# Running sums moved under the projections, decays read from padded buffers, and the scan's inverse begun by direction

## Chip, core and metric

One core of a Trainium2 chip runs the whole program: TensorE (PE, with its weight loads as PEld), VectorE (DVE), ScalarE (ACT), GpSimd (POOL) and SyncE (SP), which work in parallel and wait for one another by semaphores. The metric is the device time of one execution in microseconds; lower is better. All data is float32.

## What is computed

Two layers of a transformer block with three mixers, then one block of another kind, on 256 tokens of width 1024 with 256 context tokens. The change lies in the second block's recurrence. Cut to what matters:

```
z = centred_shift(z, shift_w)               # a three-token blend per channel
r, k, v, wd, ad, gd = split(z)
w_log = -softplus(-(w0 + tanh(wd) @ w_up)) - 0.5      # per direction
decay = exp(-exp(w_log))
a     = sigmoid(a0 + ad @ a_up)                       # per direction
kk    = head_l2norm(k * k_k);  k_eff = k * (1 + (a - 1) * k_a)
def step(s, (w, kk, a, k, v, r)):           # 16 heads of 64, forward and backward in time
    sa = s @ kk
    s  = s * w - outer(sa, kk * a) + outer(v, k)
    return s, s @ r
```

Four steps' worth of context tokens (64 each) and then four of the input's tokens are scanned; only the latter give an output. Since exp(-exp(w_log)) is exp(-c * sigmoid(..)) with c = exp(-0.5), the product of decays over a span of tokens is the exponential of a running sum of sigmoids.

## The kernel before

The recurrence is computed in chunks of 64 tokens: eight steps h = 0 to 7, each with both directions d (0 forward, 1 backward) side by side in 1024 columns (2 directions x 8 channel blocks x 64 tokens). Steps 4 to 7 are X_STEPS, which also read the state. A step solves a triangular system of 64 x 64 per head and direction, by an inverse that doubles its block size in six levels (LEVELS).

**Projections.** RW_ORDER lists 26 chunks p = 0 to 25 of 128 channels. For each, TensorE multiplies (`rw_chunk`), ScalarE evacuates twice (L2182, L2183), VectorE adds the two shifted neighbours (L2593, L2595). Chunks 2 to 9 are 256 columns wide, 10 to 25 are 512. Behind chunks 4 to 19 stand the 16 rate products (`rates`, n = p - 4): two banks of TensorE, two sigmoids of ScalarE (L2158) into `staged`. After each odd n ScalarE issues two stores (L2163) of that pair to `rates_dram`, and the next pair's sigmoids wait for them, since `staged` has one buffer. Chunks 13 and 17 give VectorE the squares of the keys (`kk_squares`), chunks 15 and 19 the reciprocals of their norms (`kk_inverse_roots`, L2585). PSUM is two rings of four banks, one that ScalarE empties (`act_ring`) and one that VectorE empties (`dve_ring`); TensorE's `open` waits until the bank's last user is done, and `rates` opens two banks before its first product.

**Loading.** Once all 16 stores have landed, SP loads the rates of steps 0 and 1 (L1524), and later those of step h when step h-2 has made its matrices. R0 holds the decay sigmoids of a step, R1 the others.

**A step.** VectorE makes the inclusive running sum of R0 in r2 (`cumulate`, L2560) and the exclusive one, the difference, in r3 (`exclude`). ScalarE turns them into three exponentials: R0 (`first_decays`, L2168), r2 (L2172) and r3 (L2175). GpSimd multiplies them with the keys into Pm, Qm and Km (`removal_raw`, `key_factors`, `removal_keys`, `keys_raw`, `keys`; all L2939). All of this is made for step h+1 during step h; for step 0 during chunks 20 to 25. TensorE then multiplies removal and keys (`together`), VectorE masks the result to LT (`left_matrix`) and Apk (`intra`), ScalarE evacuates the token halves (L2218), GpSimd subtracts the identity (`begin_inverse`) and makes ARm, ScalarE copies its halves crosswise to DTm (`first_transposed`). TensorE makes the right-hand sides U0 (`uncorrected`), which ScalarE evacuates (L2206), in steps 4 to 7 the products Arq and Ark (`reads`), and then runs `inverse`: an identity product per direction, and five rounds of left products and doubled products, in banks held for its whole length. The four banks of the products are those that K and U0 had before.

The order is written out by hand: each engine runs its own list.

## Time and profile before

| what | us |
|---|---|
| median of the runs (lowest, highest of 3) | 2798.57 (2788.01, 2801.04) |
| the profiled execution | 2783.9 |
| its span on the core | 2782.1 |
| TensorE busy | 2546.2 (92%) |
| VectorE, ScalarE, GpSimd busy | 1305.2, 607.6, 510.3 |
| granted TensorE clock, mean | 0.967 |

Busy time is the sum of an engine's instructions; the rest of its span it waits. A granted clock of 1 is 2.4 GHz. In a timeline a row is a run of like instructions: start, time, engine, line of the kernel, operation, tiles, count, and in brackets the idle time before it with what ended it ("<-ACT mem L2206": an instruction of ScalarE at that line; "ACTq" or "DVEq": a drain or semaphore of its queue; "issue": nothing that the profile shows). The projections for the recurrence end at about 1526 us, the scan at about 1936.

### The profile page before, as it was taken

The numbers are of one execution on the slowest core, as the hardware profiler recorded it, in microseconds if no ns is written. First come the engines' busy times: TensorE is split into PE (matmuls) and PEld (weight loads), VectorE is DVE, ScalarE is ACT, GpSimd is POOL, SyncE is SP. The second block draws the span as 40 slices with busy tenths as digits, with TensorE's granted clock in tenths as the row PEclk, the third lists the DMA queues.
The fourth block names the chain that finished last, engine by engine and source line by source line (L and its number), as shares of the span: only waits on it lengthen the run. The fifth ranks groups of instructions, "written<-read, shape, count | busy, mean of one in ns | idle before, by whom it ended". The sixth has DMA issues, their size and how long they took to land.

```text
span 2782.1 us, 51515 instructions
## 1 busy us (share of the span) xinstructions
PE 2546.2 (92%) x22060; PEld 1751.8 (63%) x22060; DVE 1305.2 (47%) x2861; ACT 607.6 (22%) x1348; POOL 510.3 (18%) x402
## 2 busy tenths in 40 slices
PE   8999999999999999998899788898998988877777
PEld 6688785477887844444677788888876533333333
DVE  2873300147631002066347445544217677777666
ACT  2253000014320000115233344332001111111111
POOL 0000000000000000000003544440002454545452
PEclk9999999999999999999999899999999998989999
DMA  5423343343234346215442000002337999999997
GB/s 197 154 96 121 148 155 152 132 172 123 92 121 152 151 151 263 115 61 212 140 132 61 33 17 33 18 3 96 126 127 308 411 420 421 421 421 422 421 421 312
DMA packets 76642, 523.81 MB, mean 188 GB/s; under 512 B 6704, under 2 KB 23088, under 8 KB 28848
## 3 DMA queue, kind: packets, MB, share of 16 engines
q0 software_dynamic: 37056, 269.12, 23.4%
q1 hardware_dynamic: 22768, 243.80, 23.0%
q10 hardware_dynamic: 16640, 8.39, 1.1%
q8 instruction: 126, 2.06, 0.3%
q14 instruction: 52, 0.43, 0.0%
HBM read 511.85 MB, written 9.44 MB: 187 GB/s over the span
## 4 chain that ended last, share of the span: by engine, by line
PE 72%; DVE 12%; DMA 10%; issue 2%; DVEq 2%; ACT 2%; ACTq 0%; POOL 0%; SPq 0%
PE psum L519 35%; PE psum L1562 28%; DMA mem<-weights,mem 8%; PE psum L2007 4%; DVE mem L2889 4%; DVE mem L2393 2%; PE psum L746 2%; PE psum L535 1%; PE psum L1979 1%; DMA rates_dram<-mem 1%; PE psum L1572 1%; DVEq L2514 0%; DVE mem L2847 0%; DVE mem L2530 0%; DVEq L2563 0%
## 5 line engine op out<-in xcount | busy, mean ns | idle before, releaser
L1562 PE MATMUL psum<-mem 64*64 64x64 f32 (+5 forms) x16032 | 935.2, 262 | 78.4 <-ACT mem L2206 17.8
L519 PE MATMUL psum<-mem 128*128 128x256 f32 (+9 forms) x4228 | 966.9, 398 | 4.2 <-ACTq L803 2.1
L1562 PEld LDWEIGHTS psum<-mem 64*64 64x64 f32 (+2 forms) x16032 | 737.6, 147 | 275.1 <-issue 150.6
L519 PEld LDWEIGHTS psum<-mem 128*128 128x128 f32 (+4 forms) x4228 | 706.5, 182 | 256.9 <-issue 168.6
L2007 PE MATMUL psum<-mem 128*128 128x512 f32 x1024 | 496.5, 642 | 124.7 <-ACT mem L2357 121.8
L2007 PEld LDWEIGHTS psum<-mem 128*128 128x128 f32 x1024 | 205.5, 205 | 409.2 <-issue 244.7
L3028 POOL DMA_INDIRECT mem<-weights,mem x256 | 318.3, 1243 | 531.3 <-PE psum L2007 265.7
L2889 DVE CUSTOM_DVE_ANT_0 mem<-mem 128x1024 f32<-128x1024 f32 x256 | 307.4, 1224 | 139.5 <-DMA mem<-weights,mem 132.9
L2939 POOL TENSOR_TENSOR mem<-mem 128x512 f32<-128x512 f32 (+2 forms) x132 | 186.0, 1427 | 649.2 <-PE psum L1562 462.5
L2393 DVE TENSOR_TENSOR mem<-psum,mem 128x512 f32<-128x512 f32 (+1 forms) x193 | 131.0, 683 | 264.7 <-PE psum L1562 239.6
L2393 DVE TENSOR_TENSOR mem<-mem 128x4 f32<-128x4 f32 (+7 forms) x219 | 147.5, 681 | 89.3 <-ACTq L2115 67.5
L2352 ACT ACTIVATE mem<-mem 128x4 f32<-128x4 f32 (+2 forms) x70 | 14.4, 205 | 513.1 <-DVE mem L2893 504.3
L1259 DVE TENSOR_TENSOR mem<-mem 128x512 f32<-128x512 f32 x32 | 22.2, 692 | 193.7 <-ACTq L961 193.7
L1050 DVE SCALAR_TENSOR_TENSOR mem<-mem 128x256 f32<-128x256 f32 x240 | 105.6, 481 | 9.0 <-issue 0.4
L1262 DVE TENSOR_TENSOR mem<-psum,mem 128x512 f32<-128x512 f32 x8 | 5.5, 692 | 205.5 <-PE psum L519 205.5
L1275 POOL DMA_DIRECT2D mem<-vectors x1 | 0.5, 536 | 544.3 <-DVEq L1266 544.3
L1277 POOL MEMSET mem<- 128x256 f32 x1 | 0.3, 311 | 502.0 <-ACT mem L964 502.0
L2357 ACT ACTIVATE mem<-mem 128x128 f32<-128x128 f32 x256 | 82.5, 390 | 32.6 <-DVE mem L2393 31.2
L815 ACT ACTIVATE mem<-psum 128x512 f32<-128x512 f32 (+5 forms) x94 | 48.5, 569 | 105.8 <-PE psum L519 101.8
L960 ACT ACTIVATE mem<-psum 128x512 f32<-128x512 f32 x32 | 19.1, 597 | 201.6 <-PE psum L519 201.6
L2258 ACT ACTIVATE mem<-psum 128x512 f32<-128x512 f32 x64 | 38.2, 597 | 113.0 <-PE psum L1562 110.4
L746 PE MATMUL psum<-mem 128*128 128x512 f32 x128 | 57.5, 608 | 3.8 <-DVEq L1248 3.8
(242 smaller groups left out, 1294.7 us busy)
## 6 DMA issues: line engine op xcount, KB each, us to landing
mem<-weights SPq DMA_DIRECT2D x100, 2048.0 KB, 7.4
rates_dram<-mem ACTq DMA_DIRECT2D x16, 512.0 KB, 7.1
mem<-rates_dram SPq DMA_DIRECT2D x16, 512.0 KB, 5.0
mem<-weights SPq DMA_DIRECT2D x7, 1024.0 KB, 6.8
mem<-weights SPq DMA_DIRECT2D x2, 2176.0 KB
mem<-weights,mem POOLq DMA_INDIRECT x256, 27.2
mem<-weights SPq DMA_DIRECT2D x2, 1536.0 KB, 8.0
mem<-weights SPq DMA_DIRECT2D x2, 1152.0 KB
```

The source lines that it names most:

```text
L519: ins = pe.matmul(out, lhsT, rhs, start=start, stop=stop, skip_group_check=skip)
L746: ins = pe.matmul(b, mg[:, k, t * P:(t + 1) * P], w[half][:, k, :], start=k == 0, stop=k == 7)
L815: return A(dst, src(b) if src else b, func).then_inc(act_ring.free, 1)
L1050: v.scalar_tensor_tensor(cacc[:, c, :], src, w, cacc[:, c, :], ALU.mult, ALU.add)
L1562: ins = pe.matmul(out, lhsT, rhs, start=start, stop=stop, skip_group_check=skip)
L2007: last = pe.matmul(psum[:, 4 + 2 * t + half, :], diag[:, n % DIAGS, :], rows_uv[buf_of[n]][:, D + half * 512:D + (half + 1) * 512], start= ...
L2258: A(Dm[:, d * 512:(d + 1) * 512], banks[2 * d], ACT.Copy)
L2357: A(diag[:, n % DIAGS, :], ident, ACT.Copy, scale=g1[:, n:n + 1]).then_inc(diag_ready.sem, 1)
L2393: return v.tensor_tensor(o, a, b, op)
L2889: v.tensor_tensor_reduce(u, u, h2[:, t, :], 1.0, 0.0, ALU.mult, ALU.add, actp[:, n:n + 1])
L2939: return pool.tensor_tensor(o, a, b, op)
L3028: pool.indirect_dma_start(out=rows_uv[buf_of[n]], out_offset=None, in_=UV, in_offset=bass.IndirectOffsetOnAxis(ap=eidx_u[:, n:n + 1], axis ...
```

## The change

The change does the following. The running sums are made where the sigmoids are staged: VectorE runs one `tensor_tensor_scan` in place per chunk (two rate chunks of one part at a time), two chunks behind the sigmoids; there are two staging buffers, and GpSimd issues the stores once both sums of a pair exist. What the scan loads is already the running sum; its buffers are 65 columns apart and have a column of ones in front of (or behind) each 64, so that the exclusive decay is the inclusive one read one column away. Each step keeps two exponentials, and r3 is gone. In a step GpSimd, ScalarE and TensorE treat the inverse's first level by direction.

```diff
-    rates_in = [sb2(2048, slots_at), lora]
-    R0, R1 = ([buf[:, 1024 * part:1024 * part + 1024] for buf in rates_in] for part in range(2))
-    first_restart = r3[:, 0:512]
-    staged = [yb.rearrange("p c t -> p (c t)")[:, 1024 * part:1024 * part + 1024].rearrange("p (b c n) -> p b c n", b=8, c=2)
-              for part in range(2)]
+    rates_in = [sb2(2 * RATES, slots_at).rearrange("p (s n) -> p s n", s=2), rates_odd.rearrange("p (s n) -> p s n", s=2)]
+
+    def padded(ap, at):
+        return ap[:, at:at + 1040].rearrange("p (d c n) -> p d c n", d=2, n=65)[:, :, :, 0:64]
+
+    R0, R1 = ([padded(buf[:, part, :], 1) for buf in rates_in] for part in range(2))
+    R0_before = [[padded(buf[:, 0, :], 2 * d)[:, d, :, :] for d in range(2)] for buf in rates_in]
+    staging = [yb.rearrange("p c t -> p (c t)"), zv[:, 4:8, :].rearrange("p c t -> p (c t)")]
+    staged = [[buf[:, 1024 * part:1024 * part + 1024].rearrange("p (b c n) -> p b c n", b=8, c=2) for part in range(2)]
+              for buf in staging]
     rates_dram = nc.dram_tensor("rates_dram", (2, 8, P, 2, 8, 64), F32, kind="Internal").ap()
     at_kt = rtop[0] - 7 * 1024
...
@@ -1520,9 +1527,9 @@
                         sp.wait_ge(*intra_ready.at(h - 2, 1))
                     for d in range(2):
                         stream, step = divmod(h, 4)
-                        to = rates_in[h % 2].rearrange("p (s d n) -> p s d n", s=2, d=2)[:, :, d, :]
-                        sp.dma_start(to, rates_dram[d, 4 * stream + (3 - step if d else step)].rearrange("p s c n -> p s (c n)")).then_inc(
-                            rates_landed[h % 2], 16)
+                        for part, to in enumerate((R0, R1)):
+                            sp.dma_start(to[h % 2][:, d, :, :], rates_dram[d, 4 * stream + (3 - step if d else step), :, part]).then_inc(
+                                rates_landed[h % 2], 16)
...
         def reads(h):
-            b = [[dve_ring.open(pe, n) for n in ("Arq", "Ark")] for _ in range(2)]
+            b = []
+            pe.wait_ge(*lt_ready.at(h, 1))
             for d in range(2):
+                b.append([dve_ring.open(pe, n) for n in ("Arq", "Ark")])
+                pe.wait_ge(*qt_ready.at(h, d))
...
-        def inverse(h):
+        def first_left(h, d, left):
+            pe.wait_ge(*inverse_begun.at(h, d))
+            for c in range(8):
+                for head in range(2):
+                    last = tile(left[d], d, c, head, 0, 0, half_of(LT), lambda side, d, c: C2["id2"][64 * side:64 * side + 64, :])
+            last.then_inc(left_full.sem, 1)
+
+        def inverse(h, left):
             products = [[act_ring.open(pe, "held") for _ in range(2)] for _ in range(2)]
-            left = [dve_ring.open(pe, "held") for _ in range(2)]
-            pe.wait_ge(*inverse_begun.at(h))
-            for d in range(2):
-                for c in range(8):
-                    for head in range(2):
-                        last = tile(left[d], d, c, head, 0, 0, half_of(LT), lambda side, d, c: C2["id2"][64 * side:64 * side + 64, :])
-                last.then_inc(left_full.sem, 1)
-            pe.wait_ge(*inverse_begun.at(h, 1))
...
@@ -1921,11 +1931,18 @@
                 pe.wait_ge(*qt_ready.at(h, 0))
                 together(removal(h, 1), keys(h, 0))
                 together(keys(h, 1))
-            pe.wait_ge(*qt_ready.at(h, 1))
-            uncorrected(h)
             if h in X_STEPS:
                 reads(h)
-            inverse(h)
+                uncorrected(h)
+                left = [dve_ring.open(pe, "held") for _ in range(2)]
+                first_left(h, 0, left)
+            else:
+                left = [dve_ring.open(pe, "held") for _ in range(2)]
+                first_left(h, 0, left)
+                uncorrected(h)
+            pe.wait_ge(*qt_ready.at(h, 1))
+            first_left(h, 1, left)
+            inverse(h, left)
@@ -2150,34 +2167,30 @@
 
         def rates(n):
             d, c = divmod(n, 8)
-            if n >= 2 and c % 2 == 0:
-                act.wait_ge(rates_stored, 16 * n)
+            pair = n // 2
+            if pair >= 2 and c % 2 == 0:
+                act.wait_ge(rates_stored, 32 * (pair - 1))
             for part, bias in enumerate(("w0", "a0")):
                 b = take("rate").rearrange("p (b n) -> p b n", b=8)
                 k = 8 * d + c
-                done(A(staged[part][:, :, c % 2, :], b, ACT.Sigmoid, bias=V2[bias][:, k:k + 1]))
-            if c % 2:
-                act.drain().then_inc(rates_staged.sem, 1)
-                act.wait_ge(*rates_staged.at(0, n // 2))
-                for part in range(2):
-                    act.dma_start(rates_dram[d, :, :, part, c - 1:c + 1, :].rearrange("b p c n -> p b (c n)"),
-                                  staged[part].rearrange("p b c n -> p b (c n)")).then_inc(rates_stored, 16)
-
-        def first_decays(h):
-            act.wait_ge(*cumsum_ready.at(h))
-            A(R0[h % 2], r2, ACT.Exp, scale=DECAY)
+                done(A(staged[pair % 2][part][:, :, c % 2, :], b, ACT.Sigmoid, bias=V2[bias][:, k:k + 1]))
+            act.drain().then_inc(rates_staged.sem, 1)
+
+        def decays(h):
+            act.wait_ge(rates_landed[h % 2], 64 * (h // 2 + 1))
+            if h:
+                act.wait_ge(*k_ready.at(h - 1))
+            sums = R0[h % 2].rearrange("p d c n -> p (d c) n")
+            A(ch(r2), sums, ACT.Exp, scale=-DECAY)
             act.drain()
-
-        def removal_decays():
-            A(r2, r2, ACT.Exp, scale=-DECAY)
-
-        def key_decays():
-            A(r3, r3, ACT.Exp, scale=DECAY).then_inc(decays_ready.sem, 1)
+            A(sums, sums, ACT.Exp, scale=DECAY).then_inc(decays_ready.sem, 1)
...
+            if p == 22:
+                act.wait_ge(rates_stored, 16 * STORES)
             dst, w = shift_out(c)
             A(dst, b[:, HALF - w:HALF], ACT.Copy, scale=V2["shift"][:, 26 + c:27 + c])
             done(A(zraw[:, p % 2, HALF - w:HALF], b[:, HALF - w:HALF], ACT.Copy))
...
             key_tokens(h, 1)
-
-        def first_transposed(h):
-            act.wait_ge(*inverse_begun.at(h, 0))
-            A(DTm[64:128, :], ARm[0:64, :], ACT.Copy)
-            A(DTm[0:64, :], ARm[64:128, :], ACT.Copy)
-            act.drain().then_inc(inverse_begun.sem, 1)
-
-        def inverse(h, between):
+            if h in X_STEPS:
+                first_transposed(h, 0)
+            first_transposed(h, 1)
+
+        def first_transposed(h, d):
+            act.wait_ge(*inverse_begun.at(h, d))
+            half = slice(512 * d, 512 * d + 512)
+            A(DTm[64:128, half], ARm[0:64, half], ACT.Copy)
+            A(DTm[0:64, half], ARm[64:128, half], ACT.Copy)
+            act.drain().then_inc(inverseT_ready[d].sem, 1)
+
+        def inverse(h):
             banks = act_ring.held(4)
             for j in range(1, LEVELS):
                 for d in range(2):
...
@@ -2547,27 +2552,24 @@
         def dir_(ap, d):
             return ch2(ap)[:, d, :, :]
 
-        def restarts(to):
-            v.memset(to, 1.0)
-            v.drain()
-            v.memset(to.rearrange("p (c t) -> p c t", c=8)[:, :, 0:1], 0.0)
-            v.drain()
-
-        def cumulate(h, d, restart=restart):
-            s = slice(512 * d, 512 * d + 512)
-            r0 = R0[h % 2]
-            out, decay = (r2[:, s][:, ::-1], r0[:, s][:, ::-1]) if d else (r2[:, s], r0[:, s])
-            v.tensor_tensor_scan(out, restart, decay, 0.0, ALU.mult, ALU.add)
-
-        def exclude(h):
-            v.drain()
-            tt(r3, r2, R0[h % 2], ALU.subtract)
+        def restarts():
+            v.memset(restart, 1.0)
+            v.drain()
+            v.memset(restart.rearrange("p (c t) -> p c t", c=8)[:, :, 0:1], 0.0)
+            v.drain()
+
+        def cumulate(n):
+            pair, part = divmod(n, 2)
+            v.wait_ge(*rates_staged.at(0, 2 * pair + 1))
+            sums = staging[pair % 2][:, 512 * part:512 * part + 512]
+            sums = sums[:, ::-1] if pair >= 4 else sums
+            v.tensor_tensor_scan(sums, restart, sums, 0.0, ALU.mult, ALU.add)
             v.drain().then_inc(cumsum_ready.sem, 1)
 
         def chunk_decay(h):
             v.wait_ge(*decays_ready.at(h))
-            v.tensor_copy(Wnext[:, 0:8], dir_(R0[h % 2], 0)[:, :, 63])
-            v.tensor_copy(Wnext[:, 8:16], dir_(R0[h % 2], 1)[:, :, 0])
+            v.tensor_copy(Wnext[:, 0:8], R0[h % 2][:, 0, :, 63])
+            v.tensor_copy(Wnext[:, 8:16], R0[h % 2][:, 1, :, 0])
             v.drain()
 
         def kk_squares(half):
...
+                cumulate(n)
+            if n == 14:
+                cumulate(14)
+                cumulate(15)
             if p == 20:
                 v.wait_ge(weights.used, used0 + SLOTS + ITEM2["rw4_0"] + 1)
-                restarts(first_restart)
-                v.wait_ge(rates_landed[0], 32)
-                cumulate(0, 0, first_restart)
-                cumulate(0, 1, first_restart)
-            if p == 21:
-                exclude(0)
-            if p == 23:
+                for buf in rates_in:
+                    v.memset(buf[:, 0, 0:520].rearrange("p (c n) -> p c n", n=65)[:, :, 0:1], 1.0)
+                    v.memset(buf[:, 0, 521:1041].rearrange("p (c n) -> p c n", n=65)[:, :, 64:65], 1.0)
+            if p == 24:
                 chunk_decay(0)
-            if p == 24:
                 v.memset(yb, 0.0)
                 v.memset(St, 0.0)
         v.drain().then_inc(state_ready.sem, 1)
...
                 ptt(ch2(LT)[:, d, :, :], ch2(LT)[:, d, :, :], bc(C2["id2"], 1, 8), ALU.subtract)
-            pool.drain()
-            if h:
-                pool.wait_ge(*u_ready.at(h - 1, 1))
-            for d in range(2):
+                pool.drain()
+                if h and d == 0:
+                    pool.wait_ge(*u_ready.at(h - 1, 1))
                 ptt(ch2(ARm)[:, d, :, :], ch2(LT)[:, d, :, :], bc(first[:, d, :], 1, 8), ALU.mult)
-            pool.drain().then_inc(inverse_begun.sem, 1)
-
+                pool.drain().then_inc(inverse_begun.sem, 1)
+
+        for pair in range(8):
+            d, c = divmod(2 * pair, 8)
+            pool.wait_ge(*cumsum_ready.at(0, 2 * pair + 1))
+            for part in range(2):
```

VectorE at chunks 14 and 15 of the projections, before; L2593 and L2595 are the two shifted additions, L2585 the reciprocals, L2393 a product:

```order
L2593 SCALAR_TENSOR_TENSOR mem<-mem 128x2x255 [waits shift_parts_ready]
L2595 SCALAR_TENSOR_TENSOR mem<-mem 128x2x255
L2593 SCALAR_TENSOR_TENSOR mem<-mem 128x2x255 [waits shift_parts_ready]
L2595 SCALAR_TENSOR_TENSOR mem<-mem 128x2x255
L2585 RECIPROCAL mem<-mem 128x512 [waits kk_root_ready,dve_bank_full] x4
L2393 TENSOR_TENSOR mem<-mem 128x2048
```

The same place after; L2566 is a running sum (printed as a SCALAR_TENSOR_TENSOR), L2595 and L2597 are the additions:

```order
L2595 SCALAR_TENSOR_TENSOR mem<-mem 128x2x255 [waits shift_parts_ready]
L2597 SCALAR_TENSOR_TENSOR mem<-mem 128x2x255
L2566 SCALAR_TENSOR_TENSOR mem<-mem 128x512 [waits rates_staged]
L2595 SCALAR_TENSOR_TENSOR mem<-mem 128x2x255 [waits shift_parts_ready]
L2597 SCALAR_TENSOR_TENSOR mem<-mem 128x2x255
L2587 RECIPROCAL mem<-mem 128x512 [waits kk_root_ready,dve_bank_full] x4
L2398 TENSOR_TENSOR mem<-mem 128x2048
L2566 SCALAR_TENSOR_TENSOR mem<-mem 128x512 [waits rates_staged]
```

A running sum stands behind each chunk's additions; that of chunk 15, the second of pair 4, also behind the reciprocals.

TensorE in step 1, from the second removal product with the first keys to the inverse's loop, before; 64x2x64 are removal and key products:

```order
L1562 MATMUL psum<-mem 64x2x64 [waits act_bank_free]
L1562 MATMUL psum<-mem 64x2x64 x15
L1562 MATMUL psum<-mem 64x64 [waits act_bank_free,state_ready,intra_ready,qt_ready]
L1562 MATMUL psum<-mem 64x64 x15
L1562 MATMUL psum<-mem 64x64 [waits term_full,tokens_ready]
L1562 MATMUL psum<-mem 64x64 x31
L1562 MATMUL psum<-mem 64x64 [waits term_full]
L1562 MATMUL psum<-mem 64x64 x15
L1562 MATMUL psum<-mem 64x64 [waits dve_bank_free,act_bank_free,inverse_begun]
L1562 MATMUL psum<-mem 64x64 x31
L1880 UNCONDITIONAL_BRANCH [waits inverse_begun]
```

And after:

```order
L1569 MATMUL psum<-mem 64x2x64 [waits act_bank_free]
L1569 MATMUL psum<-mem 64x2x64 x15
L1569 MATMUL psum<-mem 64x64 [waits inverse_begun,dve_bank_free]
L1569 MATMUL psum<-mem 64x64 x15
L1569 MATMUL psum<-mem 64x64 [waits state_ready,act_bank_free]
L1569 MATMUL psum<-mem 64x64 x15
L1569 MATMUL psum<-mem 64x64 [waits term_full,intra_ready,tokens_ready]
L1569 MATMUL psum<-mem 64x64 x31
L1569 MATMUL psum<-mem 64x64 [waits term_full,intra_ready]
L1569 MATMUL psum<-mem 64x64 x15
L1569 MATMUL psum<-mem 64x64 [waits inverse_begun,qt_ready]
L1569 MATMUL psum<-mem 64x64 x15
```

The identity products (16 for each direction) stood together behind U0 and needed the product banks (act_bank_free); now the first 16 stand before U0's 64, the other 16 behind, and the product banks are opened last.

ScalarE at chunks 5 and 6, before; L2158 are the sigmoids:

```order
L2158 ACTIVATE mem<-psum,mem 128x8x64 [waits act_bank_full] x2
L2163 DMA rates_dram<-mem 128x8x128 [waits rates_staged]
L2163 DMA rates_dram<-mem 128x8x128
L2182 ACTIVATE mem<-psum,mem 128x256 [waits shift_parts_used,act_bank_full]
L2183 ACTIVATE mem<-psum 128x256
L2158 ACTIVATE mem<-psum,mem 128x8x64 [waits act_bank_full,rates_stored]
```

And after, from chunk 6 to chunk 8; L2176 are the sigmoids, L2195 and L2196 the evacuations:

```order
L2176 ACTIVATE mem<-psum,mem 128x8x64 [waits act_bank_full] x2
L2195 ACTIVATE mem<-psum,mem 128x256 [waits shift_parts_used,act_bank_full]
L2196 ACTIVATE mem<-psum 128x256
L2176 ACTIVATE mem<-psum,mem 128x8x64 [waits act_bank_full] x2
L2195 ACTIVATE mem<-psum,mem 128x256 [waits shift_parts_used,act_bank_full]
L2196 ACTIVATE mem<-psum 128x256
L2176 ACTIVATE mem<-psum,mem 128x8x64 [waits act_bank_full,rates_stored]
```

The stores left ScalarE's list for GpSimd's, where each pair waits for both running sums of its pair; the first sigmoids that wait for `rates_stored` are those of chunk 8.

## Rows read from the trace of the kernel before

**Rows 1.** The page's chain that ended last, shares of the span by engine
```profile
PE 72%; DVE 12%; DMA 10%; issue 2%; DVEq 2%; ACT 2%; ACTq 0%; POOL 0%; SPq 0%
```

**Rows 2.** Stages: us, then busy us (and count) of PE, PEld, DVE, ACT, POOL, granted clock, DMA
```profile
1330.00:1526.00 196.00, 185.12 (x797) 141.94 (x795) 93.53 (x83) 64.94 (x105) 22.20 (x16) 0.97 0.37 118
1526.00:1936.00 410.00, 351.79 (x13446) 333.74 (x13446) 197.78 (x263) 156.12 (x232) 166.39 (x117) 0.94 0.07 23
```

**Rows 3.** TensorE's timeline: start, busy us, line, xcount [idle before <-releaser]
```profile
1379.74 12.65 PE L1562 MATMUL psum<-mem 64*128 64x512 f32 x40 [4.13 <-ACT mem L2158]
1394.78 131.27 PE L1562 MATMUL psum<-mem 64*128 64x512 f32 x572 [2.39 <-ACT mem L2158]
```

**Rows 4.** Landing of the two stores issued at 1397.3 and of those at 1466.3
```profile
DMA to landing us min/median/max: 8.9/9.4/10.0
...
DMA to landing us min/median/max: 3.3/4.0/4.7
```

**Rows 5.** Scan step 2, timelines of VectorE, ScalarE and TensorE
```profile
1634.79 0.69 DVE L2393 TENSOR_TENSOR mem<-psum,mem 128x512 f32<-128x512 f32 x1 [0.32 <-PE psum L1562]
1635.60 3.97 DVE L2560 TENSOR_TENSOR_SCAN mem<-mem 128x512 f32<-128x512 f32 x2
...
1648.77 0.69 DVE L2393 TENSOR_TENSOR mem<-psum,mem 128x512 f32<-128x512 f32 x1 [0.67 <-PE psum L1562]
...
1642.07 1.31 ACT L2206 ACTIVATE mem<-psum 128x512 f32<-128x512 f32 x2
...
1635.98 1.15 PE L1562 MATMUL psum<-mem 64*64 64x64 f32 x32 [1.23 <-ACTq L2223]
...
1643.69 7.79 PE L1562 MATMUL psum<-mem 64*64 64x64 f32 x222 [3.73 <-ACT mem L2206]
```

**Rows 6.** A window of TensorE alone: us, busy (x), granted clock, DMA, GB/s
```profile
1644.00:1648.00 4.00, 4.00 (x88) 0.50 0.01 4
```

**Rows 7.** Scan steps 4 and 5, timelines of VectorE and TensorE
```profile
1760.94 2.33 DVE L2570 COPY mem<-mem 128x8 f32<-128x8 f32 x1
...
1785.21 1.50 DVE L2393 TENSOR_TENSOR mem<-psum,mem 128x512 f32<-128x512 f32 x2 [0.22 <-issue]
...
1798.76 0.69 DVE L2393 TENSOR_TENSOR mem<-psum,mem 128x512 f32<-128x512 f32 x1 [0.55 <-PE psum L1562]
...
1787.41 1.15 PE L1562 MATMUL psum<-mem 64*64 64x64 f32 x32 [3.23 <-ACTq L2223]
1788.72 5.68 PE L1562 MATMUL psum<-mem 64*64 64x64 f32 x218 [0.16 <-PE psum L1562]
```

**Rows 8.** DMA issues by GpSimd, gathers and one plain: ns min/median/max
```profile
L3028 POOL DMA_INDIRECT mem<-weights,mem x256: 939/947/1989, 2115.0 to 2743.9; - x128
...
L1275 POOL DMA_DIRECT2D mem<-vectors x1: 536/536/536, 552.6 to 552.6; - x1
```

**Rows 9.** VectorE's timeline at chunks 13, 15 and 19
```profile
1430.45 4.66 DVE L2393 TENSOR_TENSOR mem<-mem 128x2048 f32<-128x2048 f32 x2
...
1460.30 2.29 DVE L2393 TENSOR_TENSOR mem<-mem 128x2048 f32<-128x2048 f32 x1
...
1496.39 2.29 DVE L2393 TENSOR_TENSOR mem<-mem 128x2048 f32<-128x2048 f32 x1
```

**Rows 10.** ScalarE's timeline at chunks 17 and 19
```profile
1463.63 0.69 ACT L2182 ACTIVATE mem<-psum,mem 128x512 f32<-128x512 f32 x1 [4.71 <-PE psum L1562]
...
1479.95 0.69 ACT L2182 ACTIVATE mem<-psum,mem 128x512 f32<-128x512 f32 x1 [5.55 <-PE psum L1562]
```

**Rows 11.** GpSimd's timeline, products of step 0
```profile
1499.03 11.40 POOL L2939 TENSOR_TENSOR mem<-mem 128x256 f32<-128x256 f32 x8 [441.79 <-PE psum L1562]
1512.80 5.99 POOL L2939 TENSOR_TENSOR mem<-mem 128x1024 f32<-128x1024 f32 x5 [2.38 <-ACT mem L2175]
1518.97 5.25 POOL L2939 TENSOR_TENSOR mem<-mem 128x512 f32<-128x512 f32 x3 [0.18 <-issue]
```

**Rows 12.** TensorE's timeline, values and keys of step 0
```profile
1529.41 5.66 PE L1562 MATMUL psum<-mem 64*64 64x64 f32 x160 [0.91 <-DVE mem L2595]
```

82 lines of the change are left out of this document (38 added, 44 removed).

## The prediction

> **What bounds the kernel now.** I read the page's chain first, then the stage table, then the chain of waits and each engine's timeline of two stages. The chain is 72% TensorE, 12% VectorE and 10% DMA [rows 1], so a saving counts only where TensorE waits. The change touches two stages: the last projections (about 1330 to 1526 us) and the eight scan steps (1526 to 1936). TensorE is busy 185 of 196 us in the first, and 352 of 410 in the second [rows 2]. So little is to be won in the projections and some 58 us stand open in the scan.
>
> In the projections the only long idle times of TensorE are 4.1 and 2.4 us, both ended by the sigmoids of L2158 [rows 3]; these had waited for the store of the pair before. A pair of stores lands 10.4 us after its first issue while weights stream (10.0 and 0.4 between the two issues), and 5.1 (4.7 and 0.4) in the quiet later part [rows 4]. In a scan step the place to look is the beginning of the inverse. In step 2 VectorE has the second half matrix at 1634.8, then makes two running sums (4.0) and their difference; ScalarE may evacuate U0 only behind the exponential that needs them, at 1642.1; TensorE stands 3.7 us and begins at 1643.7, and the first level-1 product comes at 1648.8 [rows 5]. The clock granted to TensorE from 1644 to 1648 is 0.50, its lower level of 1.2 GHz, right after that idle time [rows 6].
>
> **The scan, part by part.** Removed per step: two running sums (4.0) and their difference on VectorE, one 1024-wide exponential of ScalarE (two are left, 1.06 each, now both behind U0). Moved: in steps 0 to 3 TensorE runs the first identity product of direction 0 between the K products and U0, the other behind U0; in steps 4 to 7 the reads come ahead of U0.
>
> Steps 0 to 3, on step 2's rows: the K products end at about 1634.7 (VectorE takes the second at 1634.8 [rows 5]). The identity product takes 1.1 and ends at 1635.8; its input has long been there, because GpSimd no longer holds direction 0 back for direction 1. U0's 64 products take 4.0 (from 1636.0 until the idle time before 1643.7 begins, 1640.0 [rows 5]), so 1639.8; the second identity product ends at 1640.9, the first level's left product at 1642.0. ScalarE in that time has key tokens, half transposes, removal tokens, key tokens, half transposes: 3 x 0.6 and, estimated by the same number of elements in a lane, 4 x 0.6; with the waits between from 1634.6 to 1639.2, then U0 to 1640.6, just in time. So the product that came at 1648.8 comes at 1642.2: 6.6 us a step. I take 6.5 for each of four, 26 us; step 0 waits longer before and may give 8. Bounds: 3.7 (only the idle time goes) and 8.
>
> Steps 4 to 7, on step 5's rows: from the intra matrix to the level-1 product it is 13.6 us, 1785.2 to 1798.8 [rows 7]. Reads and U0 take 7.0 together there, from 1787.4 to 1794.4 [rows 7]. After: reads 3.0, U0 4.0, two identity products 2.2, a left product 1.1, and 0.9 for the tokens that the second half of the reads waits for: 11.3. That is 2.3 a step, 9 us over four; bounds 1 and 3.5. Once, at 1760.9, a tiny copy of VectorE took 2.33 us, beside GpSimd's products [rows 7]; those will be over by then: 2 us. Scan in all: minus 37.
>
> What hides the rest: GpSimd's products for the next step need the decays, which now come at about 1643 and not 1659, so they end some 12 us earlier; nobody waited for them. The loads in pieces of 64 columns, 4 DMAs a step and not 2, have a step of 47 us to land. I cost both at nothing; if the loads took over 45 us they would end every wait of a step.
>
> **The projections, part by part.** Added on VectorE: 16 running sums of 2.1 us with drain, one behind each of chunks 6 to 19 and two behind 20. The stores go from ScalarE's queue to GpSimd's and leave only after the second sum of a pair. There are two staging buffers, so pair k+2 waits for the store of pair k. That sounds like more slack, but the sum adds two chunks of delay: the sums of pair k end in chunk 7+2k, and chunk 8+2k wants that store landed. So the distance from store to need is again under one chunk, and now VectorE's other work stands in it.
>
> The price of a pair's store from GpSimd isn't in the trace. From below: the quiet pair, 5.1 us. From above: a gather's issue takes 947 ns for 128 rows [rows 8]; at that rate the 1024 rows of a store take 7.6 us, two 15.2, and landing 4.7: 20. A plain issue with 128 rows takes 0.54 [rows 8]. I take 7.5 us, the quiet pair and 1.2 us for each issue, because the plain row is the nearest one; the bounds are kept for the range.
>
> - Up to chunk 15: one stall of TensorE (chunk 9) in the place of two, then a small one at chunk 15, where the squares of chunk 13 (4.7 us [rows 9]) precede a sum. I take +3, bounds -3 and +8.
> - Chunk 15 to 17: VectorE's reciprocals and the product behind them end at 1462.6 [rows 9]; the second sum of pair 4 comes behind them. 1462.6 + 2.1 + 7.5 + 1.3 for the sigmoids that wait = 1473.5, where ScalarE began chunk 17 at 1463.6 [rows 10]: +9.9. TensorE stands here for some 12 us, since it opens both rate banks at once.
> - Chunk 17 to 19: 1.5 evacuation and signal, 1.6 shifts, 4.7 squares, 2.1 sum, 7.5 store, 1.3 sigmoids = 18.7, against 1479.95 - 1463.63 = 16.3 [rows 10]: +2.4. Sum +15.3.
> - Chunk 19 to the scan: VectorE ended the product of chunk 19 at 1498.7 [rows 9], now 1514.0; sum 2.1, shifts 1.7, the last two sums 4.1: 1521.9. Store 7.5, 1529.4. Only then SP loads step 0: four issues and a landing, 8 us (4 x 1.9 + 0.4; a quiet pair of stores of as many rows takes 5.1), 1537.4. GpSimd's products for step 0 follow: 11.4 + 6.0 + 5.2 + 0.2 [rows 11] = 22.8, so the keys are ready at 1560.2. Before they were ready at 1524.2, hidden under projections, and TensorE wanted them at 1529.4 + 2.1 = 1531.5 [rows 12]. +28.7.
> - TensorE will have stood idle before that; 4 us at half clock cost 2 [rows 6]. +31 in all.
>
> So the cover of step 0's preparation (1.8 us of slack at 1526) is gone, and the chain VectorE, store, load, GpSimd sets the start of the scan. Three stores lie on it (pairs 4, 5, 7): each us more in a store costs 3.
>
> **Sum.** +31 - 37 = -6 us on the profiled execution's 2783.9 (its span of 2782.1 and 1.8 around it). That one lies 0.5% under the median of 2798.57 (2788.01 to 2801.04). I forecast for the median: 2792.
>
> **A rule against the change.** At 1760.9 VectorE's copy stretched from 0.17 to 2.33 us beside GpSimd [rows 7], so the two engines do get in each other's way; a store issued by GpSimd beside VectorE isn't in the trace. The Trainium skill (SBUF — State Buffer, "Who interferes with whom") says that VectorE in a two-port mode starves GpSimd's writing of descriptors, and that a transfer to be hidden under VectorE belongs on ScalarE's or SP's queue. By that rule the stores wait for VectorE's work behind the sums; whether sums and shifts are such operations no row here shows.
>
> The skill's fit for such a DMA (DMA: Bandwidth & Descriptors, "Anatomy of one DMA") is 2.0 us + bytes/436e3, 3.2 us for 512 KB; the quiet rows show 3.3 and 4.7. By it the pair would be nearer 5 than 7.5.
>
> **Rivals.**
> - Quick stores: pairs land in 5.1 us. Three times 2.4 less: -13.5, 2785. For it: the quiet landings [rows 4]; against it: GpSimd writes 1024 rows each.
> - Slower than before: GpSimd's writing of rows. From 12 us a pair the chain gives +13.5 more (+7.5 in all), from 14.5 us it is over 0.5% slower; at 16 us +25.5 more, 2818; at 20 us 2830. For it: 7.4 ns a row in the gather [rows 8]; against it: the plain row. Starved stores have the same place: if GpSimd waits for what VectorE does behind each of three sums (shifts 1.6 and a sum 2.1, some 4 us), it is +12, 2804. The skill's rule above is this case.
> - The scan gives back only idle time: U0's evacuation is again last, or GpSimd's second direction. Then 4 x 3.7 + 4 x 1 + 2 = 21 and not 37: +10, 2808.
> - The pre-scan chain binds less than I think, for example since TensorE and ScalarE run ahead: +15 and not +31: -22, 2776.
>
> **Chances.** Forecast case 0.38 (its own range 2782 to 2803), quick stores 0.22, slow stores or starved ones 0.15, scan gives less 0.12, weak pre-scan chain 0.13. About 0.5%, 14 us, is what can be told from no change, so the bounds are 2784.6 and 2812.6. Faster: weak chain 0.12, half of quick stores 0.11, a seventh of the forecast case and the luckier part of the rest 0.14, together 0.37. Slower: slow stores 0.11, a share of the scan case 0.04, tail of the forecast case 0.03: 0.18. Same 0.45. Range 2768 to 2818: the slow case at 16 us, the weak chain with a scan gain of 45.
>
> **What would show it.** Right: TensorE idle for about 12 us near chunk 17, ended by the sigmoids; the last store landed near 1529 and not 1493; step 0's keys at 1555 to 1565, TensorE idle before; intra to level 1 in 7 us in steps 0 to 3 and 11 in 4 to 7; clock near 1.0 at the inverse's start. Wrong: GpSimd issues over 2 us each, a first scan product before 1545, TensorE idle for over 2 us at U0 or at the second identity product, or waits on the rates' landing in the scan.

## The result: 0.8% faster, and the profile after

The changed kernel takes 2769.5 us in the median of ten runs (2762.3 to 2783.7), the kernel before, run in turn with it, 2794.5 (2784.1 to 2801.0). The ratio is 0.992, its 95% interval 0.9903 to 0.9938. The forecast was 2792, "same" by its likeliest case. The time lies in the range of 2768 to 2818 by only 1.5 us, and outside the likeliest case's own 2782 to 2803: that it was not missed altogether is in part luck. Measured by the forecast's own mark of 0.5% (2784.6) the change is faster, to which it gave 0.37.

The profiled execution has a span of 2760.4 us. Its stages answer to [rows 2], with the windows' bound at 1541, since the scan starts later (columns: us, busy us and count of PE, PEld, DVE, ACT, POOL, granted clock, DMA share, GB/s):

```profile
1330.00:1541.00 211.00, 187.76 (x827) 145.13 (x827) 106.45 (x105) 65.62 (x107) 29.73 (x31) 0.96 0.35 110
1541.00:1920.00 379.00, 342.22 (x13454) 323.35 (x13451) 161.07 (x239) 150.74 (x239) 153.92 (x118) 0.99 0.12 30
```

The clock of the scan is the thing to see: 0.99 where it was 0.94. To compare more than two kernels I use two stretches with ends that each of them has: P, from ScalarE's tanh in chunk 2 to VectorE's copy of the chunk decay in step 0 (128x16), and S, from that copy to the last output that is added in step 7.

| | tanh | P | S | rest |
|---|---|---|---|---|
| before | 1353.3 | 177.4 | 404.5 | 847.0 |
| after | 1352.8 | 190.4 | 369.5 | 847.6 |
| predicted change | | +31 | -37 | |
| measured change | | +13.0 | -35.0 | |

So the scan gave about what was forecast, and the projections cost less than half. The 369.5 is the lowest of five kernels with this scan, though; the others have 373.8 to 374.9 (below), so the gain is 30 to 35 us. TensorE's timeline in the projections, for [rows 3] and [rows 12] (start, busy us, xcount, [idle before <-releaser]):

```profile
1388.27 70.45 PE L1569 MATMUL psum<-mem 64*128 64x512 f32 x296 [3.81 <-ACT mem L2176]
1466.15 64.80 PE L1569 MATMUL psum<-mem 64*128 64x512 f32 x276 [7.43 <-ACT mem L2176]
1538.58 9.65 PE L1569 MATMUL psum<-mem 64*64 64x128 f32 x224 [7.63 <-POOLq L2970]
```

One stall of 3.8 us stands where there were 4.1 and 2.4; a new one of 7.4 us at chunk 17 and one of 7.6 us before step 0's first products. ScalarE's timeline shows the sigmoids waiting for the store, for [rows 10] (evacuation of chunk 15, sigmoids of chunk 16, evacuations of 17 and 19):

```profile
1439.25 0.69 ACT L2195 ACTIVATE mem<-psum,mem 128x512 f32<-128x512 f32 x1 [0.17 <-issue]
...
1465.32 1.26 ACT L2176 ACTIVATE mem<-psum,mem 128x512 f32<-128x512 f32 x2 [13.55 <-DMA rates_dram<-mem]
1466.75 0.69 ACT L2195 ACTIVATE mem<-psum,mem 128x512 f32<-128x512 f32 x1 [0.17 <-issue]
...
1484.85 0.69 ACT L2195 ACTIVATE mem<-psum,mem 128x512 f32<-128x512 f32 x1 [1.73 <-PE psum L1569]
```

VectorE at chunk 15 (as in [rows 9], now with the running sum behind the product), and GpSimd's last stores and first products, for [rows 8] and [rows 11]:

```profile
1455.69 2.29 DVE L2398 TENSOR_TENSOR mem<-mem 128x2048 f32<-128x2048 f32 x1
1457.89 1.22 DVE L2566 TENSOR_TENSOR_SCAN mem<-mem 128x512 f32<-128x512 f32 x1
```

```profile
1505.33 1.76 POOL L2997 DMA_DIRECT2D rates_dram<-mem  x2 [27.58 <-DVEq L2567]
1509.50 0.89 POOL L2997 DMA_DIRECT2D rates_dram<-mem  x1 [2.41 <-DVEq L2567]
1513.82 0.89 POOL L2997 DMA_DIRECT2D rates_dram<-mem  x1 [3.43 <-issue]
1524.74 2.62 POOL L2940 TENSOR_TENSOR mem<-mem 128x256 f32<-128x256 f32 x4 [10.03 <-issue]
1527.61 10.86 POOL L2940 TENSOR_TENSOR mem<-mem 128x512 f32<-128x512 f32 x9 [0.25 <-issue]
1538.65 4.63 POOL L2940 TENSOR_TENSOR mem<-mem 128x512 f32<-128x512 f32 x3 [0.18 <-issue]
```

An issue takes 0.89 us, a running sum 1.22. The 16th store leaves 3.43 us behind the 15th, and GpSimd waits for nothing that the profile shows. The line of all GpSimd stores gives the time to landing, for [rows 4]:

```profile
DMA to landing us min/median/max: 3.8/5.0/8.7
```

In the scan, step 2 answers to [rows 5] (VectorE's first intra matrix and first level-1 product; ScalarE's evacuation of U0, now ahead of the exponentials of L2184; TensorE's stretch with the second identity product):

```profile
1631.10 0.69 DVE L2398 TENSOR_TENSOR mem<-psum,mem 128x512 f32<-128x512 f32 x1 [0.21 <-issue]
...
1640.47 0.69 DVE L2398 TENSOR_TENSOR mem<-psum,mem 128x512 f32<-128x512 f32 x1 [2.27 <-PE psum L1569]
...
1636.85 1.31 ACT L2217 ACTIVATE mem<-psum 128x512 f32<-128x512 f32 x2
1638.32 1.06 ACT L2184 ACTIVATE mem<-mem 128x1024 f32<-128x1024 f32 x1 [0.17 <-issue]
...
1638.59 1.11 PE L1569 MATMUL psum<-mem 64*64 64x64 f32 x31 [1.14 <-DVEq L2681]
```

From the first intra matrix to level 1 it is 9.4 us. Before it was 15.0, from 1633.78 to the 1648.77 of [rows 5]; VectorE's first intra matrix before:

```profile
1633.78 0.69 DVE L2393 TENSOR_TENSOR mem<-psum,mem 128x512 f32<-128x512 f32 x1 [0.22 <-issue]
```

In the changed kernel the clock behind it is full, where [rows 6] had 0.50:

```profile
1640.00:1644.00 4.00, 2.98 (x126) 2.55 (x125) 1.38 (x2) 1.59 (x3) 3.71 (x5) 1.00 0.02 4
```

Step 5 takes 10.7 us for the same stretch, 1770.56 to 1781.24, where [rows 7] gave 13.6. Step 4 did not gain (14.8 us, before 13.4). TensorE's timeline and the windows around it:

```profile
1721.06 0.80 PE L1569 MATMUL psum<-mem 64*64 64x64 f32 x39 [0.15 <-PE psum L1569]
1723.84 9.53 PE L1569 MATMUL psum<-mem 64*64 64x64 f32 x249 [1.98 <-issue]
```

```profile
1720.00:1724.00 4.00, 1.87 (x75) 1.62 (x74) 1.29 (x2) 1.93 (x4) 0.00 (x0) 0.93 0.98 203
1724.00:1728.00 4.00, 3.92 (x83) 3.77 (x85) 0.00 (x0) 1.50 (x3) 0.97 (x1) 0.50 0.06 11
```

TensorE stands for 2 us on nothing that is shown while the DMA engines are 98% busy with the rates of step 6, and then works for 4 us at its lower level, 1.2 GHz.

### The profile page after: what moved, and what is told of

Same layout as the page of the kernel before. It is cut to its first block and busy times, and to the rows that moved or that the text cites. A ratio compares the mean times of both kernels' runs of the same rounds, so it can differ in the third digit from the quotient of the medians.

```text
span 2760.4 us, 51595 instructions
## 1 busy us (share of the span) xinstructions
PE 2531.2 (92%) x22060; PEld 1739.6 (63%) x22060; DVE 1274.7 (46%) x2855; ACT 602.6 (22%) x1356; POOL 504.1 (18%) x418
## 5 line engine op out<-in xcount | busy, mean ns | idle before, releaser
L1569 PE MATMUL psum<-mem 64*64 64x64 f32 (+5 forms) x16032 | 919.0, 257 | 68.3 <-issue 14.9
L1569 PEld LDWEIGHTS psum<-mem 64*64 64x64 f32 (+2 forms) x16032 | 724.1, 143 | 262.3 <-issue 161.1
L2940 POOL TENSOR_TENSOR mem<-mem 128x512 f32<-128x512 f32 (+2 forms) x132 | 167.5, 1286 | 189.5 <-DVEq L2645 144.7
L2398 DVE TENSOR_TENSOR mem<-mem 128x512 f32<-128x512 f32 (+7 forms) x211 | 137.8, 661 | 88.9 <-ACTq L2132 67.5
L2997 POOL DMA_DIRECT2D rates_dram<-mem x16 | 14.2, 892 | 442.0 <-DVEq L2567 438.6
L960 ACT ACTIVATE mem<-psum 128x512 f32<-128x512 f32 x32 | 19.1, 597 | 201.6 <-PE psum L519 201.6
```

The costliest lines, as they stand in the source:

```text
L1569: ins = pe.matmul(out, lhsT, rhs, start=start, stop=stop, skip_group_check=skip)
L2398: return v.tensor_tensor(o, a, b, op)
L2940: return pool.tensor_tensor(o, a, b, op)
```

## The experiments

Each was timed in five rounds, but for one kernel that ran once. All values in us; P and S are of one profiled execution each. Five kernels with the changed kernel's scan, unchanged, have S from 369.5 to 374.9, so differences of S under 5 us tell nothing. P is steadier: four kernels with the changed kernel's projections have 190.4 to 193.1, three with those of before 177.4 to 179.5; here differences under 3 us tell nothing.

| kernel | ratio (95%) | P | S |
|---|---|---|---|
| changed kernel | 0.992 (0.9903 to 0.9938) | 190.4 | 369.5 |
| sums first | 0.989 (0.9866 to 0.9914) | 180.5 | 374.9 |
| sums before reciprocals | 0.9867 (0.9839 to 0.9894) | 175.1 | 374.6 |
| late loads | 0.9923 (0.9901 to 0.9946) | 191.1 | 374.2 |
| order of the inverse only | 0.9933 (0.9908 to 0.9958) | 179.0 | 390.4 |
| old inverse | 0.9997 (0.998 to 1.0014) | 190.4 | 391.1 |
| two idle sums | 0.9943 (0.9921 to 0.9966) | 193.1 | 372.6 |
| last store by SyncE | 0.9883 (0.9859 to 0.9908) | 178.9 | 374.1 |
| one store more | one run, 2763.2 us | 183.3 | 373.8 |
| split and SyncE | 0.9845 (0.9817 to 0.9872) | 177.1 | 374.9 |
| exponential behind U0 | 0.9908 (0.9883 to 0.9933) | 179.5 | 385.8 |
| two staging buffers | 0.9881 (0.9857 to 0.9906) | 167.9 | 381.3 |
| padded sums in the scan | 0.9837 (0.9815 to 0.986) | 168.6 | 378.4 |

### What cost the 13 us in the projections

**Sums first.** In VectorE's chunk, `cumulate(n)` goes ahead of the squares and reciprocals:

```diff
+            if 0 <= n < 14: cumulate(n)
             if p in (13, 17): kk_squares(...)
             if p == 15: kk_inverse_roots(0) ...
-            if 0 <= n < 14: cumulate(n)
```

> The changed kernel with VectorE's running sum of a chunk placed ahead of the squares (chunks 13 and 17) and of the reciprocals (chunks 15 and 19) instead of behind them. Theory (VectorE's place for the sum sets the store, the store the sigmoids, the sigmoids TensorE): the second sum of pair 4, now at 1457.9 us behind 15.3 us of reciprocals and product, moves to about 1443; the 7.4 us stall of TensorE at 1466 goes, and all behind it comes some 7 us earlier, the first intra product at about 1540 and not 1547; the ratio to the kernel before falls from 0.992 to 0.9895. Rival (TensorE or the weights limit this stretch anyway): the stall appears elsewhere and the scan starts within 2 us of 1547, ratio 0.992.

P fell by 9.9, and the stall at chunk 17 is gone. Expected were some 7; the other 2 are chunk 18, which took 9.9 us behind the stall (granted clock 0.50 from 1466 to 1470 in the changed kernel) and takes 8.2 here. TensorE's timeline has one piece from 1390.5 on:

```profile
1390.50 132.91 PE L1569 MATMUL psum<-mem 64*128 64x512 f32 x572 [3.94 <-ACT mem L2176]
1530.77 5.15 PE L1569 MATMUL psum<-mem 64*64 64x128 f32 x96 [7.36 <-POOLq L2972]
```

The chain is as told: VectorE's place for a sum sets the store, the store the sigmoids, these TensorE. The ratio's interval overlaps that of the changed kernel; P and the stall in the trace are what decide.

**Sums before reciprocals.** As above, and the second `kk_inverse_roots` with its product goes from chunk 19 to chunk 20, behind the last two sums:

```diff
-            if p == 19:
+            if p == 20:
                 kk_inverse_roots(1)
```

> As the kernel with the sums first, and also the reciprocals, the product and the signal for the second half of the keys (15.3 us of VectorE) moved from chunk 19 to chunk 20, behind the last two running sums. Theory (the last store and step 0's loads set the start of the scan): the last sum comes at about 1490 and not 1509, the last store lands near 1500, the loads near 1507; GpSimd then waits for the keys of VectorE (about 1508) and has step 0's keys at about 1527, and TensorE finds them ready: the 7.6 us of idle time before the first scan product go too. First intra product at about 1532, ratio 0.987. Rival (late shifts hold TensorE up): the reciprocals behind chunk 20 delay the shifts of chunks 21 to 24 by 15 us, TensorE stalls on its banks or at the values' product, and nothing is won beyond the kernel with the sums first (0.9895).

P falls to 175.1, not told apart from the 177.4 of the kernel before, and in the place of the 7.6 us stall there are waits of 2.4, 1.0 and 1.4. The rival is half right: VectorE's late shifts now lie beside GpSimd's products, and both slow down. The timelines of VectorE (two shift operations, the tiny copy) and of GpSimd:

```profile
1512.00 0.75 DVE L2595 SCALAR_TENSOR_TENSOR mem<-mem 128x510 f32<-128x510 f32 x1
...
1519.81 1.37 DVE L2595 SCALAR_TENSOR_TENSOR mem<-mem 128x510 f32<-128x510 f32 x1 [1.25 <-ACTq L2197]
...
1522.72 2.14 DVE L2571 COPY mem<-mem 128x8 f32<-128x8 f32 x1
```

```profile
1512.45 4.11 POOL L2942 TENSOR_TENSOR mem<-mem 128x256 f32<-128x256 f32 x4 [10.81 <-DVEq L2619]
```

A shift takes 0.75 us alone and 1.37 beside GpSimd, GpSimd's first four products 4.1 us and not 2.6.

**Last store by SyncE.** Sums first, and the 16th store from SyncE's queue, which stands idle there:

```diff
+                sp.wait_ge(*cumsum_ready.at(0, 15))
+                sp.dma_start(rates_dram[1, :, :, 1, 6:8, :]..., staged[1][1]...).then_inc(last_stored, 16)
```

> The kernel with the sums first, with the very last of the 16 stores issued by SyncE and not GpSimd. In three traces GpSimd issues that store 3.43 us after the one before it has been issued, in the others the two follow at once. Theory (that store stands on the path to the scan's start, store, load, products): it is issued together with its sibling, 3.4 + 0.9 us earlier, and the copy in step 0 comes 4 us earlier, 176.5 us behind the tanh and not 180.5; ratio to before 0.9875. Rival (the stores then share the DMA engines and land later, or SyncE's queue takes the time): under 1.5 us, ratio 0.989.

P is 1.6 lower than in its parent, not 4, which is under what P can tell; nor does the ratio tell the two apart. Counted from the tanh, SyncE's first load starts 2.9 us earlier, since the pair's other store now takes 5.2 us to land; 1.4 of these go in a pause between GpSimd's products (at 1516.92), which the parent doesn't have. Nearer to the rival. The expectation counts the pause of 3.43 us in three traces and not in the others. In truth every kernel whose 16 stores all come from GpSimd has it, six of six, at 3.42 to 3.44 us.

**One store more.** Sums first, and an extra store of the same shape behind pair 0's two:

```diff
+            if pair == 0:
+                pool.dma_start(spare_dram..., staged[0][1]...).then_inc(spare_stored, 16)
```

> The kernel with the sums first, with one more store of the same shape issued by GpSimd behind pair 0's two, to a tensor nobody reads. In three kernels GpSimd's 16th store is issued 3.43 us behind the end of the 15th, whatever VectorE does then. Theory (it depends on how many rows GpSimd's queue has written: 16 stores of 1024 rows): now the gap stands in front of the first store of pair 7, which is the 16th, or in front of both of its stores, and none is new in pair 0. Rival (it belongs to the last pair, what runs beside it or the code in front of it): the gap stays in front of the second store of pair 7 alone.

Neither. The pause between the stores has gone; GpSimd's row of the last pair:

```profile
1508.05 1.77 POOL L3003 DMA_DIRECT2D rates_dram<-mem  x2 [18.41 <-DVEq L2571]
```

A shorter one, 1.3 us, stands among the products of step 0 instead (at 1526.34), as in the two kernels with one store less on GpSimd (1.39). So the pause belongs neither to the 16th store nor to the last pair, and it is the same where VectorE does other things beside it; one store more or less moves it. What is left is the place in GpSimd's code: in the changed kernel the one packet of the instruction queue in the pause lies at its end, between 1512.6 and 1513.8. That fits, but it wasn't tested by itself.

**Two staging buffers** (see below for its scan) keeps the stores of the kernel before on ScalarE's queue and only stages the pairs in two buffers in turn:

```diff
-            if n >= 2 and c % 2 == 0:
-                act.wait_ge(rates_stored, 16 * n)
+            if pair >= 2 and c % 2 == 0:
+                act.wait_ge(rates_stored[pair % 2], 32 * (pair // 2))
```

> The kernel with the exponential behind U0, and the rates staged in two buffers in turn, so that ScalarE's sigmoids wait for the store of the pair before last and not for the last. Theory (TensorE's idle times of 4.1 and 2.4 us in the projections come from these waits): both go, from the tanh to the copy of step 0 it is 170 to 173 us, ratio 0.986. Rival (weights or ScalarE hold this stretch up anyway): 176 to 179 us, same time as with one buffer.

P is 167.9, the shortest of all: 11.6 below its parent, and TensorE has no idle time over 1 us at all in the chunks with rates. All of it lies between the evacuations of chunks 6 and 10: 34.2 us in the parent, 22.3 here.

### What gave the 35 us in the scan

**Order of the inverse only** is the kernel before with this half of the change, **old inverse** the changed kernel without it:

```diff
+            first_left(h, 0, left)      # steps 0 to 3: ahead of U0; 4 to 7: behind reads and U0
             uncorrected(h)
+            first_left(h, 1, left)
```

> The kernel before with only one half of the change: the inverse begun by direction (first identity product ahead of U0 in steps 0 to 3, reads ahead of U0 in steps 4 to 7, GpSimd's and ScalarE's parts by direction). The running sums, the difference and the exponential ahead of U0 stay in the scan; stores and projections are those of before. From VectorE's copy of the chunk decay in step 0 to the last output of step 7 it is 404.5 us before and 369.5 in the changed kernel. Theory (the chain sums, exponential, U0 ended last before, and only taking the exponential from it frees the order): U0 still waits for the exponential at 1642, the identity product that is moved ahead only fills a part of TensorE's idle time; the scan takes 393 to 400, a ratio of 0.996 to 0.999. Rival (the order itself is what gives): 375 to 382, ratio 0.990 to 0.993.

> The changed kernel with the inverse begun as before (U0, reads, then both identity products; GpSimd and ScalarE handle both directions together); the sums stay under the projections and the exponentials behind U0. Theory (most of the scan's 35 us come from the exponential and the sums): the scan takes 375 to 385 us from VectorE's copy in step 0 to the last output, with 190 us from the tanh to that copy as in the changed kernel; ratio to before 0.994 to 0.997. Rival (the order gives most): 392 to 400, ratio 1.000 to 1.003. If the two halves only work together, both kernels keep over 390.

S is 390.4 with the order alone (-14.1) and 391.1 with the other half alone (-13.4). With both it is -30 to -35. The theory of the first run gave the order too little (393 to 400 expected), that of the second the other half too much (375 to 385). Both stay just over the 390 that was named for "only together", but each gives 13 to 14 us alone: neither half is the cause, and the two nearly add up. Why the order alone pays is in step 2 of that kernel, timelines of VectorE, ScalarE and TensorE:

```profile
1631.94 3.15 DVE L2573 TENSOR_TENSOR_SCAN mem<-mem 128x512 f32<-128x512 f32 x2
...
1637.59 1.31 ACT L2216 ACTIVATE mem<-psum 128x512 f32<-128x512 f32 x2
...
1639.33 5.50 PE L1562 MATMUL psum<-mem 64*64 64x64 f32 x192 [2.76 <-ACT mem L2216]
```

TensorE's idle time is 2.8 us and not 3.7, one identity product is behind it already, and the two sums take 3.15 us and not 3.97, because GpSimd has finished its part for direction 0 before, and the second sum runs alone (1.19 us).

**Two idle sums.** The changed kernel, with two running sums back on VectorE behind the intra matrices of steps 0 to 6, which nobody waits for:

```diff
             intra(h)
+            for _ in range(2 if h < 7 else 0):
+                v.drain(); v.tensor_tensor_scan(spare, spare, spare, 0.0, ALU.mult, ALU.add)
```

> The changed kernel with two running sums of 512 columns put back on VectorE behind the intra matrices of steps 0 to 6, on a spare tile; nobody waits for them. Theory (what the change removed in the scan was the chain sums, exponential, evacuation of U0, not VectorE's time): VectorE waits 4.0 us behind the intra matrices for the first identity product anyway, so two sums of 1.2 to 2.0 us fit in; in all 0 to +5 us. Rival (VectorE's time itself was on the path): 7 x 2.9 to 4.0 = +20 to +28 us, ratio about 1.0. The duration of a sum: 1.2 us as in the projections if GpSimd's idleness makes the difference, since GpSimd computes nothing in this place; 2.0 us if it is the place in the scan or the direction.

S is 372.6, so the sums cost nothing that can be seen, and in each of steps 0 to 3 level 1 still comes 8.7 or 8.8 us behind the first intra matrix. (The ratio, 0.9943, isn't told apart from 0.992, and leaves room for some us either way.) VectorE's timeline of step 1 has them in the old gap, with the product 0.1 us behind them:

```profile
1607.38 3.29 DVE L2711 TENSOR_TENSOR_SCAN mem<-mem 128x512 f32<-128x512 f32 x2 [0.17 <-issue]
1610.78 0.69 DVE L2400 TENSOR_TENSOR mem<-psum,mem 128x512 f32<-128x512 f32 x1
```

The expectation was wrong in that GpSimd computes nothing here: it does, and in steps 1 to 3 the sum that runs 0.9 us beside it takes 2.0 us, the next, alone, 1.22. VectorE's 4 us a step by themselves were not the price. What waited for them may be: ScalarE's exponential, ahead of U0. If so, the sums need not leave the scan at all.

**Exponential behind U0.** The kernel before, with the new order and the first exponential behind U0:

```diff
-            if h < 7: first_decays(h + 1)
             for d in range(2): evac("U0", U0, d) ...
+            if h < 7: first_decays(h + 1)
```

> The kernel before with the inverse begun by direction, and ScalarE's first exponential of the next step put behind U0; the running sums and their difference stay on VectorE in the scan, the projections and the stores are those of before. Known so far for the scan (copy of step 0 to the last output): 404.5 before, 390.4 with the order alone, 391.1 with the sums and exponentials away alone, 369.5 to 374.9 with both. Theory (the running sums on VectorE are hidden, only the exponential in front of U0 was on the path): the scan takes 372 to 378 us, the stretch from the tanh to the copy stays at 177 to 179, ratio to before 0.988 to 0.990: the change's gain without its cost. Rival (the sums delay VectorE's first level product or the decays GpSimd needs): 382 to 390, ratio 0.992 to 0.994.

S is 385.8, and 381.3 with two staging buffers, whose scan is the same: the rival. Against the order alone, 390.4, the exponential's place gives 5 to 9 us; some 6 to 16 stay that the scan of the changed kernel (369.5 to 374.9) doesn't have.

**Padded sums in the scan** asks what they are. It has the changed kernel's padded buffers and two exponentials, the stores and staging of the kernel just above, and the running sums in the scan, in place, 520 columns with the pads, so that no difference and no third exponential is needed:

```diff
+            for d in range(2):
+                sums = rates_in[h % 2][:, 0, 521 * d:521 * d + 520]
+                sums = sums[:, ::-1] if d else sums
+                v.tensor_tensor_scan(sums, restart, sums, 0.0, ALU.mult, ALU.add)
```

> A version meant to beat all so far. From the changed kernel: the padded rate buffers, the shifted reading, the inverse by direction and the two exponentials behind U0. From the kernel before: the stores from ScalarE right behind the sigmoids (with two staging buffers in turn) and the running sums on VectorE in the scan, now in place over 520 columns with the pads, two a step and no difference. Theory (the sums on VectorE are hidden in the scan, as with the kernel that kept two idle sums: 372.6 us; what cost 8 to 12 us in the kernels with three exponentials, 385.8 and 381.3, is the difference and the third exponential): from the tanh to the copy of step 0 it is 167 to 170 us, the scan 372 to 377, in all 541 to 546 where the best so far has 549.2 and 549.7; ratio to before 0.983. Rival (the wait for the sums, VectorE behind the intra matrices, is what costs those 8 to 12): the scan takes 380 to 386 and the ratio is 0.988.

P 168.6, S 378.4, together 547.0, and a ratio of 0.9837: the lowest of the study, 0.8% under the changed kernel (the intervals don't meet), though its interval meets those of split and SyncE (0.9845, below), sums before reciprocals, last store by SyncE and two staging buffers. S lies between theory and rival.

A steadier measure than S is the time from the first intra matrix to level 1, added up over steps 0 to 3. It is 35.0 to 35.6 us in all eight kernels with the changed kernel's steps (the two idle sums and the late loads among them), 61.2 before, 45.6 with the order alone and 46.8 with the other half alone. With the order and the exponential behind U0 it is 39.5 (and 39.9 with two staging buffers), and here, with the sums still in the scan, 35.1. So at this place the order gives 15.6 us, the exponential's place 6, and the step to padded sums with all that it changes (no difference, no third exponential, the other two together) the last 4 to 5, about half of it in step 0; the sums themselves cost nothing. What is left of S against the changed kernel, 3.5 to 9 us, lies in steps 4 to 7 and between the steps, and its cause stays open. Its step 1, VectorE and ScalarE:

```profile
1615.85 3.20 DVE L2573 TENSOR_TENSOR_SCAN mem<-mem 128x520 f32<-128x520 f32 x2
1619.16 0.69 DVE L2405 TENSOR_TENSOR mem<-psum,mem 128x512 f32<-128x512 f32 x1
...
1619.97 1.31 ACT L2224 ACTIVATE mem<-psum 128x512 f32<-128x512 f32 x2
```

**Late loads.** SyncE's loads for step h+2 wait for the end of step h's inverse:

```diff
-                        sp.wait_ge(*intra_ready.at(h - 2, 1))
+                        sp.wait_ge(*inverse_done.at(h - 2, 1))
```

> The changed kernel with SyncE's loads of the rates of step h+2 released by the end of step h's inverse instead of by its second intra matrix. In the changed kernel TensorE stands 1.98 us in step 4 (ended 1723.84) for nothing that the profile shows, while these loads keep the DMA engines 98% busy (203 GB/s from 1720 to 1724), and the clock is at 0.50 behind it. Theory (the loads hold up TensorE's instruction loading): the gaps of steps 2, 4 and 5 (1.23, 1.98, 1.52) fall under 0.5 us each and the time falls by 3 to 6 us, ratio 0.990. Rival (the gap belongs to the jump from the loop to straight code; step 7 has 2.76 us without any load beside it): gaps of the same size stay, ratio 0.992 within 0.001. Loads that now come too late for the decays would show as waits on their landing and a longer time.

Step 4's pause shrank from 1.98 to 0.88 us, step 2's 1.23 is gone, and the clock behind step 4's is 1.00. TensorE's row and a window of this kernel:

```profile
1729.72 6.50 PE L1569 MATMUL psum<-mem 64*64 64x64 f32 x189 [0.88 <-issue]
```

```profile
1729.00:1733.00 4.00, 3.16 (x112) 3.05 (x114) 0.41 (x1) 1.81 (x4) 1.25 (x2) 1.00 0.02 6
```

The ten kernels with this order on TensorE and the loads in their old place have 2.0 to 3.1 us there; the other kernel with late loads (split and SyncE, below) has 0.61. So the loads do prolong the pause. But the time and S did not move: step 5's pause (1.52) and one of 3.3 us in step 7 stayed, and other steps took longer by as much. For the time the rival is right. Step 7 has no rates to load; SyncE's next weights stream in just ahead of its pause (98.8% of the DMA engines' time from 1874 to 1875.7 in the changed kernel, where TensorE stands from 1875.7 to 1878.4). Whether they prolong it wasn't tried.

**Split and SyncE.** Sums first, two of the four reciprocals of the second half ahead of the last two sums and two behind, the last store by SyncE, late loads:

```diff
             if p == 19: kk_inverse_roots(1, range(2))
             if p == 20: kk_inverse_roots(1, range(2, 4))
```

> A version meant to beat both: sums first, the last two running sums of chunk 20 between the first two and the last two reciprocals of the second half of the keys, the last store from SyncE, SyncE's loads for step h+2 released by the end of step h's inverse. Theory (start of the scan = the later of store, load, GpSimd and of VectorE's keys): sums end near 1496, stores land near 1501, loads near 1508, the keys of VectorE near 1505, GpSimd's products of step 0 end near 1527, and TensorE waits under 1 us before its first scan product; 170 to 173 us from the tanh to the copy of step 0 (175.1 with all reciprocals behind the sums), the scan 370 to 375; ratio 0.985. Rival: GpSimd and VectorE slow each other while VectorE makes up its late shifts (0.75 us each alone, 1.0 to 1.4 beside GpSimd), and nothing is won beyond 175; ratio 0.987.

Its ratio, 0.9845, is not told apart from 0.9867. In the trace nothing was won beyond the reciprocals moved as a whole: P is 177.1. GpSimd began only 0.8 us earlier (155.0 us behind the tanh, 155.8 there), and TensorE then waited 2.2 us for VectorE's shifts. The rival holds.

## Why the forecast was right in the scan and wrong before it

The likeliest case said +31 - 37 = -6; it is +13.0 - 35.0 = -22.0. The rival "the pre-scan chain binds less" said +15 and 2776 and comes nearest, though not for its reason: nothing ran ahead; the chain bound at chunk 17 and at the scan's start, where it was said to, with smaller terms. The forecast also started from a median of 2798.6 of three runs, which is 2794.5 over ten: 4 of the 22 us between forecast and time are that.

- **Up to chunk 15, +3 (-3 to +8).** This failed most, outside its bounds. ScalarE begins to evacuate chunk 15 at 1439.25, before at 1443.87: -4.6. Nearly all of it lies between the evacuations of chunks 6 and 10, before and after:

```profile
1370.94 0.47 ACT L2182 ACTIVATE mem<-psum,mem 128x256 f32<-128x256 f32 x1 [2.39 <-PE psum L1562]
...
1403.05 0.69 ACT L2182 ACTIVATE mem<-psum,mem 128x512 f32<-128x512 f32 x1 [5.82 <-PE psum L1562]
```

```profile
1370.37 0.47 ACT L2195 ACTIVATE mem<-psum,mem 128x256 f32<-128x256 f32 x1 [2.39 <-PE psum L1569]
...
1398.18 0.69 ACT L2195 ACTIVATE mem<-psum,mem 128x512 f32<-128x512 f32 x1 [7.18 <-PE psum L1569]
```

  That is 32.1 us before, 27.8 after, and 22.3 with two staging buffers on ScalarE's queue, where nothing stalls. The forecast knew the two stalls by TensorE's idle time, 4.1 and 2.4. They cost 9.8, since the clock falls behind them (0.61 from 1380 to 1388 in the kernel before). A store wait of ScalarE that TensorE doesn't feel costs nothing: the kernel before has one of 3.35 us at chunk 14, and chunk 15 comes 8.17 us behind chunk 14, as its neighbours do.
- **Chunk 15 to 17, +9.9 and 12 us of idle time.** Measured 1466.75 - 1439.25 = 27.5 against 19.8: +7.7, and 7.4 us idle. VectorE, store, sigmoids is the right chain ("sums first" removes it); the sum was taken at 2.1 us and takes 1.3 with its drain, the store at 7.5 and takes 5.9 (0.9 until the second store is issued, 5.0 from there to its landing). The "quick stores" rival, 5.1 us a pair, was nearer than the value chosen.
- **Chunk 17 to 19, +2.4.** 18.1 against 16.3: +1.8, but not by the chain that was added up. Chunk 18 took 9.9 us and not 8.2, with the clock at 0.50 behind the stall; chunk 19, whose sigmoids wait 4.0 us for the store, took 8.2 as before.
- **Chunk 19 to the scan, +15.7 (31 - 15.3, the clock's 2 within it).** Measured +7.7 (58.4 from chunk 19's evacuation to the copy, before 50.7). The loads took 7.1 and not 8, GpSimd 18.5 and not 22.8: in the kernel before VectorE was busy for 19.7 of the 25.2 us beside these products, here for 8.8 of 18.5. That this is why they are shorter is argued from the pairs above and not tested here. The last pair needed 8.1 us, of which 3.4 are the pause, and hides that a store is cheap. The last store landed near 1517.6, not 1529; the keys were ready at 1543.3, not 1555 to 1565; the first scan product came at 1538.6, ahead of the 1545 that the forecast named as a sign against itself.
- **Steps 0 to 3, 6.5 each.** From the first intra matrix to level 1 it was 16.3, 15.0, 15.0 and 15.0 us and is 8.8, 8.7, 9.4 and 8.8: 25.6 in all, where 26 were forecast. The 7 us named as a sign were counted from the second matrix; from there it is about 8.
- **Steps 4 to 7, 2.3 each.** Intra to level 1, step 5 gained 2.9 us, step 6 3.8, step 7 nothing, and step 4 lost 1.4: 5.2 in all and not 9. The pauses of 1.98 and 2.76 us stand where the gain was to be, in step 4 with 4 us at half clock behind.
- **The tiny copy, 2.** This term came out, and larger. From level 1 of step 4 to the first intra matrix of step 5 it is 39.3 us and was 42.9: 3.5 of the 4 us that the steps' beginnings leave of the 35. In the kernel before TensorE stood behind the copy of 2.33 us, and had a granted clock of 0.64 from 1764 to 1768; in the changed kernel the copy takes 0.17, TensorE doesn't stand, and the clock is 1.00. TensorE's row before:

```profile
1764.31 19.87 PE L1562 MATMUL psum<-mem 64*64 64x64 f32 x704 [1.93 <-DVEq L2673]
```

- **Costed at nothing.** That is right for the loads' landing (4.7 us) and GpSimd's earlier products; not quite for the loads beside TensorE's pause in step 4.
- **Slips in its sums.** The parts for steps 4 to 7 give 11.2 and not 11.3, and three quick stores -13.2 and not -13.5; neither matters.
- **What the forecast's reason missed.** It charged the sums, the difference and the exponential as one chain, and gave the order of the inverse no share of its own. In truth the sums cost nothing, the exponential's place gives 5 to 9 us, the difference and the third exponential some more, and the order 14 us of its own, with the exponential still ahead of U0. The 37 came out near the measured 30 to 35, but the shares behind it were not known. The clock gave part of both: 0.94 before, 0.95 and 0.96 with one half, 0.99 with both.

**Two memory users.** The rule of the Trainium skill that was weighed against the change (SBUF — State Buffer, "Who interferes with whom", starved descriptor writing) did not bite: 15 of the 16 issues took 0.89 or 0.90 us and the first 0.97, whatever VectorE did, and the store is issued when VectorE has ended its sum. The same section of the Trainium skill says that a VectorE instruction with two inputs in SBUF contends with a GpSimd instruction that reads SBUF. This case agrees: a running sum takes 1.22 us alone and, in the kernel before, up to 2.23 beside GpSimd's products. Not every such meeting costs: the first sum of the scan took 1.23 us with GpSimd busy all the while. The two lines below are of the changed kernel, where GpSimd only issues stores, and of the kernel before (duration ns min/median/max):

```profile
L2566 DVE TENSOR_TENSOR_SCAN mem<-mem x16: 1217/1218/1225, 1372.1 to 1508.0; 128x512 f32<-128x512 f32 x16
```

```profile
L2560 DVE TENSOR_TENSOR_SCAN mem<-mem x16: 1225/2028/2229, 1501.6 to 1842.1; 128x512 f32<-128x512 f32 x16
```

## What to carry to other kernels

Before work is moved off an engine, ask which instruction waits for it and what stands behind that one: here two sums of 4 us a step cost nothing by themselves, the exponential that waited for them in front of an evacuation cost 5 to 9 us over the scan, and the old order at the inverse's start 14. Work that is moved into a tight stage goes ahead of long work that nobody waits for yet, and a duration that is read beside a busy neighbour is not its duration alone. A stall of TensorE is priced by its chunk, from evacuation to evacuation, and not by its idle time, since the clock is low behind it: 6.5 us of idle time cost 9.8. A wait of another engine that leaves TensorE's pace as it is costs nothing.

## What had not been expected of the hardware

- TensorE and GpSimd pause for 1 to 3.4 us on nothing that the profile shows, at the same places of the code in kernel after kernel, but not for the same time (TensorE in step 7: 1.5 to 3.3 in the twelve kernels with the new order). The one that was tried, in step 4, got shorter when transfers were taken away from beside it (2.0 to 3.1 with them, 0.88 and 0.61 without). That these are loads of instructions is not shown.
- A running sum of 512 columns: 1.22 us alone, mostly 2.0 beside GpSimd, and up to 2.86; a copy of 8 columns: 0.17, and 2.14 and 2.33 beside GpSimd.
- A store of 512 KB from GpSimd: 0.89 us to issue, 3.8 to 8.7 from the start of the issue to landing (7.7 to 8.7 for the first four). Two at once, from two queues, took 3.7 and 5.2.
- The same code ahead of the tanh took from 1352.8 to 1367.8 us in the profiled executions of the study. A single profile's span doesn't rank two kernels 1% apart; stretches between fixed points do.
